# Token attention: the causal term on VectorE, the rotated queries in pieces, the row maxima from the sixth step on

## The reference, cut to what matters

```python
q = (rms_norm_2(c_q, mla_q_norm[j]) @ mla_w_uq[j]).reshape(b, s, N_TOK_HEADS, QK_DIM)   # 12 heads, 96 wide
q = jnp.concatenate([q[..., :QK_NOPE], apply_rope(q[..., QK_NOPE:], positions)], axis=-1)   # 64 + 32 turned
...
sc = jnp.einsum('bqhd,bkhd->bhqk', q_blk, k, preferred_element_type=jnp.float32) * scale
mask = k_pos[None, :] <= q_pos[:, None]
sc = jnp.where(mask[None, None], sc, -jnp.inf)
p = jax.nn.softmax(sc, axis=-1).astype(v.dtype)
return jnp.einsum('bhqk,bkhd->bqhd', p, v)
```

## Time and profile before

| | |
|---|---|
| Median of 3 runs | 3357.79 us (3356.38 to 3365.31) |
| The profiled execution | 3356.56 us, of it the span 3354.4 us |
| PE busy in the span | 3075.8 us, 92% |
| DVE, ACT, POOL busy | 1304.9, 976.9, 808.8 us (39%, 29%, 24%) |
| Mean granted clock of PE | 0.944 |
| Token attention | 2402.9 to 2809.8 us of the span |

### The profile page before, as it was taken

The page is one execution under the profiler, slowest core; times in us unless marked ns, Lnnn a source line. Parts: engine busy times, 40 slices in busy tenths (PEclk is TensorE's granted clock), DMA queues, the critical chain, the costliest instruction groups (busy, mean ns, idle before and its releaser), DMA issues. The chain is left out here.

```text
span 3354.4 us, 33625 instructions
## 1 busy us (share of the span) xinstructions
PE 3075.8 (92%) x14024; PEld 2304.5 (69%) x14024; DVE 1304.9 (39%) x1342; ACT 976.9 (29%) x1264; POOL 808.8 (24%) x380
## 2 busy tenths in 40 slices
PE   8899999999989888899999999898789998889886
PEld 3677777877766476688888787676456666667555
DVE  5153111333425443300000245230656664528555
ACT  3232222212134123311111344332133431337312
POOL 1222111214332122322222345322021211223100
PEclk9999999999989899899999999998799999999897
DMA  9311111252132352111111233312100001121201
GB/s 359 132 51 63 51 51 57 107 176 76 57 114 99 108 182 69 51 50 44 46 48 50 70 109 124 114 53 85 57 13 20 20 13 69 63 69 38 91 13 50
DMA packets 76485, 261.01 MB, mean 78 GB/s; under 512 B 8048, under 2 KB 12384, under 8 KB 75328
## 3 DMA queue, kind: packets, MB, share of 16 engines
q1 hardware_dynamic: 76352, 259.13, 22.0%
HBM read 207.10 MB, written 51.99 MB: 77 GB/s over the span
## 5 line engine op out<-in xcount | busy, mean ns | idle before, releaser
L277 POOL TENSOR_TENSOR w_lo_sb<-raw_w_sb,w_hi_sb 128x1024 fp32r<-128x1024 f32 x231 | 578.5, 2505 | 2052.1 <-ACT w_hi_sb L268 2052.0
L268 ACT ACTIVATE w_hi_sb<-raw_w_sb 128x1024 fp32r<-128x1024 f32 x231 | 243.1, 1052 | 437.2 <-PE ps L285 401.6
L285 PE MATMUL ps<-merged_parts_hi_sb,w_hi_sb 128*128 128x512 f32 x832 | 336.1, 404 | 22.6 <-PEq L500 12.1
L285 PE MATMUL ps<-merged_parts_lo_sb,w_hi_sb 128*128 128x512 f32 x832 | 332.1, 399 | 0.0
L285 PE MATMUL ps<-h_hi_sb,w_hi_sb 128*128 128x512 f32 x720 | 297.3, 413 | 18.2 <-PEq L872 11.2
L285 PE MATMUL ps<-h_lo_sb,w_hi_sb 128*128 128x512 f32 x720 | 289.1, 401 | 0.0
L285 PE MATMUL ps<-merged_parts_hi_sb,w_lo_sb 128*128 128x512 f32 x832 | 273.0, 396 | 0.0
L285 PE MATMUL ps<-h_hi_sb,w_lo_sb 128*128 128x512 f32 x720 | 246.1, 401 | 0.0
L285 PE MATMUL ps<-z_lo,w_hi_sb 128*128 128x512 f32 x512 | 206.3, 403 | 0.0
L285 PEld LDWEIGHTS ps<-merged_parts_hi_sb,w_hi_sb 128*128 128x128 f32 x832 | 158.2, 190 | 68.1 <-issue 18.6
L2732 DVE TENSOR_TENSOR ffn_hidden_sb<-ffn_hidden_sb,ps 128x1024 f32 x20 | 24.4, 1221 | 431.4 <-PE ps L285 431.4
(11 more groups left out here) (571 smaller groups left out, 5569.8 us busy)
## 6 DMA issues: line engine op xcount, KB each, us to landing
raw_w_sb<-in_w SPq DMA_DIRECT2D x231, 512.0 KB, 3.2
ada_w_sb<-in_ada SPq DMA_DIRECT2D x48, 512.0 KB, 7.5
inbox_sb<-gates_out SPq DMA_DIRECT2D x24, 512.0 KB, 4.1
gates_out<-outbox_sb SPq DMA_DIRECT2D x16, 512.0 KB, 2.6
inbox_sb<-sums_out SPq DMA_DIRECT2D x16, 512.0 KB, 4.7
spilled_sum<-x_sb SPq DMA_DIRECT2D x32, 256.0 KB, 2.0
x_sb<-spilled_sum SPq DMA_DIRECT2D x2, 4096.0 KB, 13.8
x_sb<-in_x SPq DMA_DIRECT2D x4, 1024.0 KB, 10.9
```

The costliest lines, as they stand in the source:

```text
L268: nc.scalar.activation(w_hi[:, n % RING].rearrange("p t m -> p (t m)"), raw_w[:, n % RAW], ACT.Copy).then_inc(w_rounded.sem, 1)
L277: nc.gpsimd.tensor_tensor(w_lo[:, n % RING].rearrange("p t m -> p (t m)"), raw_w[:, n % RAW], flat_hi, ALU.subtract).then_inc(w_split.sem, 1)
L285: mm = nc.tensor.matmul(o, wt, xs, start=start and part == 0 and xs is x_hi, stop=stop and part == 1)
```

## The change

In the code:

- The float32 mask product on PE is gone. On a diagonal block DVE waits for the score, adds the mask to the 128 columns in PSUM in place (`causal_term`), and ACT waits for that and not for PE.
- The steps of the second half run in the order s = 4, 5, 6, 7, 0, 1, 2, 3. So steps 0 to 7 of a head are the diagonal ones.
- For the tokens, weighings follow two scores later (`behind`), not one; the last two follow the last score, the last but one ahead of R.
- The maximum products of the next head follow score 5 (two of them) and scores 6 to 11 (one each). DVE takes maxima 0 to 3 between causal terms 5 to 7, then normalises the first half, then takes maxima 4 to 7.
- The three instructions that turn the next head's queries run between the causal terms 1 to 4 (for heads 0 and 1, at P as before). The rounding moves to ACT, after the exponential of step 4 (`round_turned`), and the first maximum product waits for it.
- `gating.high` stays at the ninth step.

The core of the diff:

```diff
+                blocks = ((0, 1, 2, 3), (4, 5, 6, 7, 0, 1, 2, 3))
+                steps = [(u, t, s) for u in range(U) for t in range(2) for s in blocks[t]]
...
                                 if causal and b == 0:
                                     evacuated("act", ("Q", u, 0))
-                                    evacuated("dve", ("Q", u, 0))
+                                    pe.wait_ge(*rounded_s.at(u + 1))
...
-                                        if diag:
-                                            mm = nc.tensor.matmul(ps[:, 4 + n % 2, 0:P], ident, C("mask_kq"),
-                                                                  start=False, stop=True)
...
-                                        if n > mine[0]:
-                                            weigh(n - 1)
+                                        if n - mine[0] >= behind:
+                                            weigh(n - behind)
                                         if causal and u + 1 < U:
-                                            if 2 <= n - mine[0] < 2 + CH:
-                                                maxima(u + 1, n - mine[0] - 2)
+
+                                            for b in {5: (0, 1), 6: (2,), 7: (3,), 8: (4,), 9: (5,), 10: (6,), 11: (7,)
+                                                      }.get(n - mine[0], ()):
+                                                maxima(u + 1, b)
+                                    if causal:
+                                        weigh(mine[-2])
                                     if causal and u + 1 < U:
                                         to_rows(u + 1)
                                     weigh(mine[-1])
...
+                        def round_turned(u):
+                            act.wait_ge(dve_free.sem, b_e["dve"] + after["dve"][at[("Q", u, 0)]])
+                            nc.scalar.activation(rounded(u)[0][64:96], q_of(u)[64:96], ACT.Copy).then_inc(rounded_s.sem, 1)
...
+                                        if on_diagonal[n]:
+                                            act.wait_ge(*causal_s.at(diagonals[n]))
+                                        else:
+                                            act.wait_ge(pe_s.sem, val(i, len(steps), b_s + n + 1))
...
+                                        if causal and u + 1 < U and n == step_at[(u, 1, 4)]:
+                                            round_turned(u + 1)
...
+                            def turn_queries(u, piece):
+                                j = at[("Q", u, 0)]
+                                q_ = q_of(u)[64:96]
+                                if piece == 0:
+                                    dve.wait_ge(pe_done.sem, base + j + 1)
+                                    nc.vector.tensor_tensor(q_, pair[j % 2][64:96], rot[64:96], ALU.mult)
+                                if piece == 1:
+                                    link(nc.vector.tensor_tensor(t_b[64:96], pair[j % 2][96:128], rot[96:128], ALU.mult))
+                                if piece == 2:
+                                    nc.vector.tensor_tensor(q_, q_, t_b[64:96], ALU.add).then_inc(dve_free.sem, 1)
+                                    dve.wait_ge(dve_free.sem, b_e["dve"] + after["dve"][j])
+
+                            def causal_term(n):
+                                dve.wait_ge(pe_s.sem, b_s + n + 1)
+                                nc.vector.tensor_tensor(ps[:, 4 + n % 2, 0:P], ps[:, 4 + n % 2, 0:P], C("mask_kq"), ALU.add
+                                                        ).then_inc(causal_s.sem, 1)
...
-                                    nc.vector.tensor_copy(rounded(u)[0][64:96], q_).then_inc(dve_free.sem, 1)
...
+                                        for j in range(CH):
+                                            causal_term(step_at[(u, 0, 0)] + j)
+                                            if 1 <= j <= 3 and 1 < u + 1 < U:
+                                                turn_queries(u + 1, j - 1)
+                                            if u + 1 < U:
+                                                for b in {5: (0, 1), 6: (2,), 7: (3,)}.get(j, ()):
+                                                    take_maxima(i, u + 1, b)
                                     normalise(i, u, 0)
-                                    if between:
-                                        for b in range(2, CH):
+                                    if causal and u + 1 < U:
+                                        for b in range(4, CH):
                                             take_maxima(i, u + 1, b)
```

More of the change, by code:

```diff
@@ L3001, in attention @@
             if causal:
-                steps = [(u, t, s) for u in range(U) for t in range(2) for s in range(4 * t + 4)]
-                last = lambda t: 4 * t + 3
+                blocks = ((0, 1, 2, 3), (4, 5, 6, 7, 0, 1, 2, 3))
+                steps = [(u, t, s) for u in range(U) for t in range(2) for s in blocks[t]]
+                begins = lambda t: 4 * t
+                last = lambda t: 3
             else:
                 steps = [(u, t, s) for u in range(U) for t in range(2) for s in range(keys_n // P)]
+                begins = lambda t: 0
                 last = lambda t: keys_n // P - 1
             step_at = {st: n for n, st in enumerate(steps)}
+            on_diagonal = [causal and s >= 4 * t for _, t, s in steps]
+            diagonals = [sum(on_diagonal[:n + 1]) for n in range(len(steps))]
             span = lambda t, s: (max(HALF * t, P * s) if causal else HALF * t, HALF * (t + 1))
@@ L3081, in body @@
                             reached = {"act": -1, "dve": -1}
+                            behind = 2 if causal else 1
                             def reads_of(e, value):
@@ L3108, in weigh @@
                                 pe.wait_ge(act_p.sem, val(i, len(steps), b_p + n + 1))
-                                if s == 0 and (g >= 2 or i is not None):
+                                if s == begins(t) and (g >= 2 or i is not None):
                                     pe.wait_ge(dve_o.sem, val(i, 2 * U, b_do + g - 1))
                                 nc.tensor.matmul(ps[:, 6 + t, lo - HALF * t:HALF], v_of(u, s), pr[:, n % 4, 0:hi - lo],
-                                                 start=(s == 0), stop=(s == last(t))).then_inc(pe_o.sem, 1)
+                                                 start=(s == begins(t)), stop=(s == last(t))).then_inc(pe_o.sem, 1)
                             def turn_values(u):
@@ L3263, in body @@
                                 link.loop(i, dve_links)
[L3264 to L3275 removed]
+                            def turn_queries(u, piece):
[13 more added lines that the diff above has]
+                                                        ).then_inc(causal_s.sem, 1)
+                            for kind, u in seq:
+                                if kind == "P" and u < 2:
+                                    for piece in range(3):
+                                        turn_queries(u, piece)
                                 if kind == "A":
@@ L3290, in body @@
                                 if kind == "S":
-                                    between = range(2) if causal and u + 1 < U else ()
-                                    for b in between:
-                                        take_maxima(i, u + 1, b)
+                                    if causal:
+                                        for j in range(CH):
[5 more added lines that the diff above has]
+                                                    take_maxima(i, u + 1, b)
                                     normalise(i, u, 0)
-                                    if between:
-                                        for b in range(2, CH):
+                                    if causal and u + 1 < U:
+                                        for b in range(4, CH):
                                             take_maxima(i, u + 1, b)
@@ L3315, in attention @@
                 stream["slot"] += U * iters
[L3316 removed]
+                over([(row_s, 16 * U), (row_in, 16 * U), (causal_s, diagonals[-1]), (rounded_s, U)])
         def memory_branch(layer, qm, Z, pairs=None, behind=(), pairs_scope=None):
```

25 lines of the change are left out of this document (9 added, 16 removed).

## The result

The changed kernel took 3370.99 us (median of 6 runs, 3370.06 to 3375.88) against 3358.15 for the kernel before beside it (6 runs, 3355.1 to 3365.31): a ratio of 1.0038 with an interval of 1.0025 to 1.0051. It is slower by 12.8 us, a little past the 0.3% (10 us) that I had set as the limit of "no change", and the interval reaches to both sides of that limit. 3362 was forecast, 9 too low; the range of 3350 to 3373 holds the time, by 2 us. "Slower" had 0.22 of my chances, "within 0.3%" 0.66.

What follows compares the result with a forecast made beforehand. TensorE was taken as the bound. Odd heads +7.7, even heads 0.0, start -2.0, heads 0, 10 and 11 -0.3, -0.65, -0.35 gave +4.4 on 3356.56, or 3361.0; set against the runs' median, forecast 3362, range 3350 to 3373.

Steps and rivals of the forecast that it cites:

- The hold of piece 2: DVE's third query-turning instruction waits for GpSimd's low part of the gated tile in five odd heads: +1.53 each, +7.7.
- h11.1: Time of the first maximum product in odd heads, in us since that head's score of step 0 began.
- The new waits: TensorE waits per head: 0.2 at score 2, 1.5 first maximum product, 1.1 seventh, 0.8 row product.
- The old waits: TensorE's waits in the kernel before, expected to go: 0.75 at the first maximum product, 1.0 at the fifth.
- Rival (b): Waits vanish through the two-score lag and a shorter chain: some 38 us less, 3320, or 3340 with half; chance 0.12.
- The causal term: DVE's 128x128 mask addition into PSUM, taken as 0.29 us, between bounds of 0.13 and 0.345.
- Rival (d): Causal terms at their bounds, -3 or +1.5; at twice the value +8, 3370; far above bounds or unseen wait 0.13.
- The clock: TensorE's granted clock in heads 1 to 9, taken to stay 1.00 despite a 3.0 us wait in odd heads.
- rival (c): The 3 us wait lowers TensorE's clock in five odd heads, 1.9 or more each: +9.5, 3371.5; chance 0.09.
- The start: Before head 0's first score: ACT's rounding, 1.7 shorter than DVE's, brings the first maxima forward; -2.0 taken.
- The sum: Even heads 0.0, odd +7.7, start -2.0, head 0 -0.3, head 10 -0.65, head 11 -0.35: +4.4.

Runs made afterwards that it cites:

- experiment 2: Changed kernel with useless float32 products on TensorE ahead of the first maximum product, two in odd heads, one in even; 3362.40 us, ratio 1.0012.
- Experiment 6: Kernel of experiment 1 with the causal term back on TensorE as a float32 product of identity and mask; 3361.17 us, ratio 1.0004.
- 7: Experiments 1 and 4 combined, plus first two pieces behind causal term 1, fifth maximum before normalisation, row product behind last weighing; 3337.75 us, ratio 0.9940.
- experiment 8: As 7, but the first half is normalised in two parts of 256 columns, either side of the fifth maximum; 3326.86 us, ratio 0.9910.
- experiment 10: Kernel before without its float32 mask products, the mask of the maximum products zero at the same cost; 3339.91 us, ratio 0.9951.
- experiment 11: Changed kernel, but ACT copies the turned values of head 0 before rounding that head's queries and weights; 3373.48 us (one run).
- experiment 12: Experiment 8 with the start of experiment 11, and SyncE sending the first row ahead of head 1's weight load; 3324.73 us, ratio 0.9901.
- experiment 1: Changed kernel, but GpSimd's low part of the gated tile waits until ACT has rounded the next head's queries; 3356.02 us, ratio 0.9995.
- experiment 4: Changed kernel with ACT rounding the turned queries after the exponential of step 3 instead of 4; 3357.26 us, ratio 0.9983.

## Why the prediction was right, and where it was not

**The hold of piece 2: right.** Predicted 2.7 us in the odd heads, 1.22 in the others; measured 2.62 and 1.22. Predicted first maximum product at h11.1 there (9.6 + 1.53), measured h11.03. Its cost by experiment 2 is 1.3 a head against 1.53: the held piece ended at h8.89 and not h9.05, and the free one at h7.63 and not h7.52. The rule of the Trainium skill (SBUF — State Buffer, "Who interferes with whom") names the pair and the winner rightly; its full block would have made the piece end 1.22 behind GpSimd, and the traces show 1.07 and 1.08.

**The new waits: right, a little large.** In head 2, predicted 0.2, 1.5, 1.1 and 0.8; measured 0.2 (score 2 at h3.74, predicted h3.77), 1.6, 0.85 and 0.6. Even heads: 31.7 predicted, 31.6 measured. Three slips of mine lie inside these figures and partly cancel. The old waits, read in the same way, were 0.65 (the first maximum product starts at 2517.36, not 2517.45) and 0.85 (2524.78 against 2523.07 + 0.86), not 0.75 and 1.0. The rounding, 1.057 behind the 8.49 of the prediction, ends at h9.55 and not h9.44, which puts the product at h9.7, and it came at h9.8. And the line through 0.68 and 1.23 gives 0.27 for a causal term and not 0.29. With the measured waits the sum of an even head is -1.76 - 0.65 - 0.85 + 0.2 + 1.6 + 0.85 + 0.6 = 0.0, and the head is 0.15 shorter than before. So the central claim stands, that what leaves TensorE comes back as waits, in DVE's chain of pieces, terms and maxima and in ACT's rounding behind it. Experiment 6 shows it from the other side (1.76 of work gone, 0.5 gained), 7 and 8 by taking the waits away. Rival (b) is out: the first maximum product starts at h9.8 and not before h8.3.

**The causal term: right.** 96 instructions of 298 ns, for the 0.29 taken; the 0.26 of the Trainium skill's first formula (VectorE: DVE Perf Modes, "The TRN2 errata") is low, its 0.29 close. Rival (d) is out.

**The clock: the step that failed.** I held the granted clock at 1.00 in heads 1 to 9, with a wait of 3.0 in the odd ones, and gave rival (c) 0.09, because it had stayed whole after 2.71 idle ahead of head 11. That one row was too thin. The windows after show 0.95 and less in all five odd heads, in two profiles, and experiment 2 prices it at 1.7 a head (1.9 for the rival). The odd heads together took 174.0 us instead of 158.8: +15.3, where +7.7 was predicted. Rival (c) gave 3371.5, which is where the kernel came out, but that it fits to 0.5 us is luck: its sum for attention is 4.4 + 9.5 = +13.9, and the profile has +20.1. What I had also not thought of: the clock fell in single even heads (+1.15 each), in head 0, which ran at half speed from 2442.0 to about 2452 (before: for about 4 us from 2445.80) and so came out 3.1 longer and not 0.3 shorter, and in head 11, which has 0.82 after 2.08 idle, less than the 2.71 that did nothing before, and came out 1.2 longer instead of 0.35 shorter. Why the clock fell in heads 0, 4 and 11 stays open; experiment 10 has the same in heads 0 and 11 of the old order.

**The start: mis-sized.** -2.0 predicted, -0.4 measured (42.36 to 41.99 from the first product to the first score). I moved the rounding to ACT without looking at what stood behind it there:

```profile
2413.32 1.05 ACT L3217 ACTIVATE q_rounded_sb<-qh_sb 32x1024 fp32r<-32x1024 f32 x1 [1.82 <-DVE qh_sb L3295]
2414.39 1.06 ACT L268 ACTIVATE w_hi_sb<-raw_w_sb 128x1024 fp32r<-128x1024 f32 x1
2415.36 0.58 ACT L3728 ACTIVATE vh_sb<-ps 128x512 f32<-128x512 f32 x1
```

```profile
2415.99 0.58 PE L3139 MATMUL ps<-k_rounded_sb,q_rounded_sb 96*128 96x256 f32 x1 [1.11 <-ACT vh_sb L3728]
```

The copy of the turned values (L3728) frees the PSUM pair of the second maximum product, and now waits for two roundings. The rows of both kernels place the whole of the missing 1.6. First the kernel before, then the changed one:

```profile
2419.64 0.45 PE L3129 MATMUL ps<-k_rounded_sb,q_rounded_sb 96*128 96x128 f32 x1 [4.72 <-DVE q_rounded_sb L3273]
...
2434.94 0.39 PE L3144 MATMUL ps<-cst_sb,att_max_t_sb 128*8 128x128 f32 x2
...
2441.85 0.29 SPq L3051 DMA_DIRECT2D att_rows<-att_neg_t_sb  x1
2444.32 0.24 SPq L3056 DMA_DIRECT2D qh_sb<-att_rows  x1
```

```profile
2414.47 0.30 PE L3139 MATMUL ps<-k_rounded_sb,q_rounded_sb 96*128 96x128 f32 x1 [3.01 <-ACT q_rounded_sb L3217]
...
2430.99 0.39 PE L3154 MATMUL ps<-cst_sb,att_max_t_sb 128*8 128x128 f32 x2
```

The stage begins at 2403.44 before and at 2400.01 after. Counted from there, the first maximum product comes at 14.46 instead of 16.20, so the 1.7 did arrive. Of it 0.83 is lost by the time that the projections of head 1 start (2422.39 against 2426.73), by the wait for L3728, and 0.39 in these projections (8.60 us to the row product against 8.21, with the clock at 0.50 for 3.1 us and not some 2.3). From the row product to the write of the row 0.48 is gained, since the negation no longer stands behind DVE's rounding. From the write to the read 0.60 is lost: 3.07 instead of 2.47, the write being issued 0.38 behind the weight load and not 0.86. That leaves 0.4. In experiment 11 the first score is 0.7 earlier, most of the 0.83; in experiment 12, with the load out of the way, the idle ahead of head 0 is 3.9 shorter than in experiment 8, so SyncE's order is worth more at this place than what the change could bring. That the closeness of the load makes the 0.60 is not tested by itself.

**The sum.** Start -0.4, head 0 +3.1, odd heads +15.3, even heads +0.5, head 10 +0.4, head 11 +1.2: +20.1 between the two profiles' attention (406.2 and 426.3), against +4.4 predicted. The profiled executions themselves differ by 3373.22 - 3356.56 = 16.7 and the medians by 12.8. The rest lies outside attention, in stages that the change does not touch: over the fourteen profiles the stage begins anywhere from 2395.5 to 2407.0. Chance is hardly all of it, though. In each of the twelve measurements of a kernel other than the one before, the median differs from that kernel by 1 to 10 us less than the profiled attention does (+12.8 against +20.1 here, -2.1 against +4 in experiment 1), always to the quick side. What causes that is not shown. So the lengths of the heads carry the argument of this document, and the medians the verdict.

## What to carry to other kernels

Work taken from the busiest engine is a gain only if what feeds that engine was not the limit at the same place: follow the chain to its next product before you count it, and look at what a moved instruction stands before on its new queue as well as behind. An instruction with two SBUF inputs on VectorE has to be placed against GpSimd's timeline, and one wait on GpSimd can be the cheapest repair. Here a wait of TensorE that grew by 1.3 us, from 1.6 to 3, cost another 1.7 in clock, so a forecast with such a wait should carry both sums with real weight. And when waits are to be taken away one by one, the busy time in the window is the floor, not the head less the waits read from start to start.

## What the runs showed of the hardware that I had not expected

- Granted clock: after 3.0 us of waiting (2.83 in the record) it fell in every odd head of two profiles of the changed kernel, after 2.1 in two odd heads of experiment 4 and not in the other three. It fell to 0.82 for head 11 after 2.08 idle, and to 0.84 after 2.76 in experiment 10, where 2.71 had left it whole. In head 4 it fell with no long wait just before, at the same place (score 2, after the turn of the values) in the changed kernel and in experiment 1. What decides this is not settled here; the idle time just ahead alone does not.
- 1.9 us of useless products in such a wait kept the clock whole in all five odd heads and made the kernel quicker (experiment 2).
- A held VectorE instruction of 1.22 us ended 1.07 or 1.08 behind GpSimd's, whatever their overlap: it took 2.62 for a start 0.81 behind a 2.35 us instruction, and 1.72 for a start 1.71 behind one.
- Copying 32x1024 float32 to fp32r took 1.05 on ACT and 2.73 on DVE.
